# One decoder block on one core: six small steps of the parameters' load, the scan, the sinks, the top-k search and the last scaled tile take other places

## Time and profile before

| | |
|---|---|
| median of three runs | 1599.07 us (1597.56 to 1600.12) |
| the profiled execution, its own time | 1598.55 us |
| its span (first to last instruction) | 1596.8 us |
| granted TensorE clock | 0.999 |
| ACT, busy | 691.2 us, 43% |
| POOL, busy | 735.4 us, 46% |
| DVE, busy | 1256.3 us, 79% |
| DMA | 385.42 MB, mean 241 GB/s |
| instructions | 25965 |

### The profile page before, as it was taken

How to read it: one execution, slowest core, us unless ns; L and a number is a source line. 1 busy time by engine, 2 the same in 40 slices (tenths; PEclk the granted TensorE clock), 3 DMA queues, 4 the chain that set the end, 5 groups by cost and what they waited for, 6 DMA issues and landing times.

```text
span 1596.8 us, 25965 instructions
## 1 busy us (share of the span) xinstructions
PE 1582.3 (99%) x9610; PEld 1394.9 (87%) x9610; DVE 1256.3 (79%) x2491; ACT 691.2 (43%) x1003; POOL 735.4 (46%) x482
## 2 busy tenths in 40 slices
PE   9999999999999999999999999999999999999998
PEld 9887777778889999999999999999999999888886
DVE  5863655644889989999588888888888888888886
ACT  6223455534434457777443333333333333333334
POOL 4774344434556566665156444545444444422210
PEclk9999999999999999999999999999999999999999
DMA  4222121434223369997999999999999999888884
GB/s 154 87 92 80 54 67 54 147 117 145 80 80 119 110 210 324 305 328 253 320 349 378 345 342 339 349 338 344 343 348 340 344 342 320 294 312 309 304 320 169
DMA packets 151393, 385.42 MB, mean 241 GB/s; under 512 B 11792, under 2 KB 61200, under 8 KB 151184
## 3 DMA queue, kind: packets, MB, share of 16 engines
q1 hardware_dynamic: 59472, 203.54, 35.4%
q0 software_dynamic: 41472, 151.01, 27.0%
q10 hardware_dynamic: 50368, 29.89, 6.1%
HBM read 355.03 MB, written 28.84 MB: 240 GB/s over the span
## 4 chain that ended last, share of the span: by engine, by line
PE 85%; POOL 4%; issue 4%; DVE 4%; DMA 2%; ACT 1%; ACTq 0%; SPq 0%; DVEq 0%; POOLq 0%
PE ps L1490 68%; PE ps L1573 5%; PE ps L1895 4%; PE ps L1510 3%; POOL wlo L507 3%; DMA vraw<-in_v 1%; POOL score L548 1%; PE ps L1849 1%; PE ps L1707 1%; PE ps L1685 0%; PE ps L1726 0%; DMA uraw<-in_uT 0%; DVE vwlo L1342 0%; DVE mtmp L1191 0%; PE ps L1597 0%
## 5 line engine op out<-in xcount | busy, mean ns | idle before, releaser
L1490 PE MATMUL ps<-hThi,uwhi 128*128 128x352 f32 x1024 | 336.5, 329 | 2.3 <-DVE uwlo L1337 1.1
L1490 PE MATMUL ps<-hTlo,uwhi 128*128 128x352 f32 x1024 | 330.7, 323 | 0.0
L1490 PE MATMUL ps<-hThi,uwlo 128*128 128x352 f32 x1024 | 330.4, 323 | 0.0
L1490 PE MATMUL ps<-vwhi,awhi 128*128 128x512 f32 x768 | 299.5, 390 | 1.2 <-DVE awlo L1360 1.1
L1490 PE MATMUL ps<-vwlo,awhi 128*128 128x512 f32 x768 | 299.7, 390 | 0.0
L1490 PE MATMUL ps<-vwhi,awlo 128*128 128x512 f32 x768 | 299.3, 390 | 0.0
L875 ACT ACTIVATE vwhi<-vraw 128x1024 fp32r<-128x1024 f32 x128 | 135.8, 1061 | 330.2 <-PE ps L1490 294.9
L598 POOL DMA_INDIRECT rows<-in_v,gidx x128 | 147.7, 1154 | 270.2 <-DVE acc L1383 253.0
L598 POOL DMA_INDIRECT rows<-in_u,gidx x128 | 178.9, 1398 | 193.0 <-DVE rows L1376 149.3
L507 POOL TENSOR_TENSOR wlo<-raw,whi 128x1024 fp32r<-128x1024 f32 x63 | 156.0, 2476 | 222.2 <-ACT whi L642 222.1
L830 ACT ACTIVATE uwhi<-uraw 128x1024 fp32r<-128x1024 f32 x128 | 135.7, 1060 | 252.7 <-PE ps L1490 243.1
(11 more groups left out here) (332 smaller groups left out, 2872.8 us busy)
## 6 DMA issues: line engine op xcount, KB each, us to landing
uraw<-in_uT SPq DMA_DIRECT2D x128, 512.0 KB, 5.3
vraw<-in_v SPq DMA_DIRECT2D x128, 512.0 KB, 5.7
raw<-in_wstream SPq DMA_DIRECT2D x70, 512.0 KB, 3.5
gmat<-gates_dram SPq DMA_DIRECT2D x64, 384.0 KB, 6.3
gates_dram<-piece ACTq DMA_DIRECT2D x11, 2048.0 KB, 13.2
xt<-in_xT SPq DMA_DIRECT2D x8, 264.0 KB, 6.0
acc<-in_x ACTq DMA_DIRECT2D x1, 2048.0 KB, 11.4
rows<-in_u,gidx POOLq DMA_INDIRECT x128, 7.1
```

The source lines that it names most:

```text
L1490: ins = pe.matmul(dst, lhs[a], rhs[b], start=first and i == 0, stop=last and i == 2)
```

## The change

- The parameters' load goes from SP's queue, where it was third, to ACT's, where it is the first instruction.
- ACT's z stage: after tile 3, tile 4's copy out of PSUM and tile 6's high part (`z_pair(2)`, k = 0) come ahead of the sigmoid of the forget gate, k = 1 behind it.
- DVE's scan of 128 x 2112 becomes two of 128 x 1056. The first waits for `w_lo` of at least 9, the second for 10, and the maximum behind them for 11 (it was 10).
- The sink column of each attention step is written by ACT instead of DVE: the one for step 0 ahead of the loop over the steps, those for steps 1 to 15 behind the exponentials of the step before. DVE's maximum waits for it through a new semaphore, `sink_ok`.
- The sum of the halves of score 14 goes from POOL to DVE, ahead of that score's search; POOL makes tile 1's low part directly behind tile 0's, then waits for that sum, and then adds score 15.
- ACT's conversion of the indices goes from ahead of tile 4's high part to behind it, ahead of `gelu(2)`.
- `scaled(0)` goes from `v` tile 124 to 125 in DVE's loop. (The other place in which `FIN_AT` stands, in ACT's loop, L973, is unchanged.)

```
--- before.py
+++ after.py
@@ -339,7 +339,7 @@
-        names = """g_first avm_ok akx_ok ones_ok par_in sink_in acc_in fin_in consts early_in early_in1 early_hi early_lo xsq_ok xadd_ok xsum_ok sd_ok rstd_ok z_copied gate_copied yhi_ok y_ok w_hi w_lo w_used z_out
+        names = """g_first avm_ok akx_ok ones_ok par_in sink_in sink_ok acc_in fin_in consts early_in early_in1 early_hi early_lo xsq_ok xadd_ok xsum_ok sd_ok rstd_ok z_copied gate_copied yhi_ok y_ok w_hi w_lo w_used z_out
@@ -381,7 +381,6 @@
         def _(sp):
             sp.dma_start(raw[:, 0, 0:EARLY], wstream[0, :, 0:EARLY]).then_inc(S["early_in"], 16)
             sp.dma_start(xt[:, 0, :], xT[:, 0, :]).then_inc(xt_in[0], 16)
-            sp.dma_start(par[:], params).then_inc(S["par_in"], 16)
             sp.dma_start(raw[:, 1, 0:EARLY], wstream[1, :, 0:EARLY]).then_inc(S["early_in1"], 16)
             sp.dma_start(xt[:, 1, :], xT[:, 1, :]).then_inc(xt_in[1], 16)
             sp.dma_start(raw[:, 0, EARLY:D], wstream[0, :, EARLY:D]).then_inc(w_in[0], 16)
@@ -566,8 +565,8 @@
                                         ).then_inc(row_in[q % SLOTS], 16)
 
             u_split(0)
-            score_sum(RS - 2)
             u_split(1)
+            pool.wait_ge(S["s_out"], RS - 1)
             score_sum(RS - 1)
             for n in range(2, U_TOP + 1):
                 if n == U_TOP - 1:
@@ -645,6 +644,7 @@
             def spans(ap):
                 return ap.rearrange("p (b x) -> p b x", b=2)
 
+            act.dma_start(par[:], params).then_inc(S["par_in"], 16)
             act.wait_ge(poo, 1)
             act.activation(rstd[:, 0:1], eps[:], ACT.Copy)
             act.wait_ge(S["early_in"], 16)
@@ -673,8 +673,8 @@
             act.wait_ge(S["lb_max"], 1)
             act.activation(lbw[:, 3:5], lbw[:, 1:3], ACT.Exp).then_inc(S["lb_exp"], 1)
 
-            def z_pair(it, dst, shift, meta):
-                for k in range(2):
+            def z_pair(it, dst, shift, meta, slots=range(2)):
+                for k in slots:
                     own = bass.ds(it * 2 + (k - shift), 1)
                     act.wait_ge(S["w_used"], it * 2 + (k + 1))
                     if meta:
@@ -696,9 +696,11 @@
 
             z_pair(1, zm, 0, True)
 
+            z_pair(2, zr, 4, False, (0,))
             act.wait_ge(S["z_out"], 4)
             act.activation(f_z, f_z, ACT.Sigmoid).then_inc(S["f_sig"], 1)
-            z_tiles(4, 8, zr, 4, False)
+            z_pair(2, zr, 4, False, (1,))
+            z_tiles(6, 8, zr, 4, False)
             z_tiles(8, 14, zm, 4, True)
             z_tiles(14, N_Z, zr, 10, False)
 
@@ -747,6 +749,15 @@
                 act.activation(oat["hi"][:, :, tt * P:(tt + 1) * P],
                                ps[:, tt % 2, :].rearrange("p (c t) -> p c t", c=4), ACT.Copy).then_inc(S["oat_hi"], 1)
 
+            def sink_column(p):
+
+                need(act, S["aexp"], 2 * p)
+                act.activation(atsc[:, :, KEYS:KEYS + 1], sink[:].rearrange("p (s c) -> p s c", s=2)[:, :, p % 4:p % 4 + 1],
+                               ACT.Copy).then_inc(S["sink_ok"], 1)
+
+            act.wait_ge(S["sink_in"], 16)
+            act.wait_ge(S["asc_mm"], 1)
+            sink_column(0)
             for i in range(HEADS + 1):
                 if i >= 5 and i % 4 == 1:
                     attention_hi(i // 4 - 1)
@@ -754,6 +765,8 @@
                     turned(i - 1)
                 if i < HEADS:
                     exponentials(i)
+                if i + 1 < HEADS:
+                    sink_column(i + 1)
                 if i == HEADS:
                     attention_hi(TT - 1)
                 for t in gate_blocks_done(gates_before(i), gates_before(i + 1)):
@@ -880,10 +893,6 @@
                 act.activation(act_w["hi"][:, m % 2, :], prod[:, m % 2, :], ACT.Copy).then_inc(S["aw_hi"], 1)
 
             for n in range(U_TOP):
-                if n == 2:
-
-                    act.wait_ge(S["tops_ok"], RS)
-                    act.activation(top_f[:], top_i[:], ACT.Copy).then_inc(S["topf_ok"], 1)
                 if n == 13:
                     act.wait_ge(S["soft"], 1)
                     act.activation(gate[:], gate[:], ACT.Exp).then_inc(S["soft_exp"], 1)
@@ -901,6 +910,10 @@
                     act.activation(tab_ji[:, 0], ps[:, 7, P:TOK].rearrange("p (t k) -> p t k", k=P), ACT.Copy).then_inc(S["tj_ok"], 1)
                 if n < U_TOP - 1:
                     u_split(n + 2, n % 2)
+                    if n == 2:
+
+                        act.wait_ge(S["tops_ok"], RS)
+                        act.activation(top_f[:], top_i[:], ACT.Copy).then_inc(S["topf_ok"], 1)
                     gelu(n)
 
 
@@ -1036,9 +1049,12 @@
             chain.done(dve.memset(starts[:], 0.0))
             chain.done(dve.tensor_copy(halves(starts[:])[:, :, 0:1], halves(f_z)[:, :, 0:1]))
             chain.done(dve.memset(halves(f_z)[:, :, 0:1], 0.0))
-            dve.wait_ge(S["w_lo"], SCAN_AT)
-            chain.done(dve.tensor_tensor_scan(flat(decay[:]), flat(f_z), flat(starts[:]), 0.0, ALU.mult, ALU.add))
-            dve.wait_ge(S["w_lo"], SCAN_AT + 1)
+            for n in range(2):
+                own = slice(n * HH // 2, (n + 1) * HH // 2)
+                dve.wait_ge(S["w_lo"], SCAN_AT + n)
+                ins = dve.tensor_tensor_scan(flat(decay[:, own]), flat(f_z[:, own]), flat(starts[:, own]), 0.0, ALU.mult, ALU.add)
+            chain.done(ins)
+            dve.wait_ge(S["w_lo"], SCAN_AT + 2)
             chain.done(dve.tensor_scalar(decay[:], decay[:], TINY, None, ALU.max))
             chain.done(dve.reciprocal(inv[:], decay[:]))
 
@@ -1134,15 +1150,13 @@
 
             def logits(p):
 
-                lo, c = P if p < 4 else 0, p % 4
+                lo = P if p < 4 else 0
                 dve.wait_ge(S["asc_mm"], p + 1)
-                if p == 0:
-                    dve.wait_ge(S["sink_in"], 16)
                 need(dve, S["aexp"], 2 * p)
-                dve.tensor_copy(atsc[:, :, KEYS:KEYS + 1], sink[:].rearrange("p (s c) -> p s c", s=2)[:, :, c:c + 1])
                 chain.done(dve.scalar_tensor_tensor(out=atsc[:, :, lo:KEYS], in0=ps[:, 6:8, lo:KEYS], scalar=HD ** -0.5,
                                                     in1=bandmask[:, lo:KEYS].unsqueeze(1).to_broadcast([P, 2, KEYS - lo]),
                                                     op0=ALU.mult, op1=ALU.add))
+                dve.wait_ge(S["sink_ok"], p + 1)
                 dve.tensor_reduce(atstat[:, 0, :], atsc[:, :, lo:KEYS + 1], AX_X, ALU.max,
                                   negate=True).then_inc(S["amax"], 1)
 
@@ -1226,6 +1240,10 @@
 
             def set_tops(n):
                 s = n % 2
+                if n == RS - 2:
+                    dve.wait_ge(S["s_half"], n + 1)
+                    dve.tensor_tensor(score[:, s], halfscore[:, s, :, 0, :], halfscore[:, s, :, 1, :], ALU.add
+                                      ).then_inc(S["s_out"], 1)
                 dve.wait_ge(S["s_out"], n + 1)
                 for tt in range(TT):
                     ins = dve.max(top_v[:, tt, n, 0:8], score[:, s, tt, :])
@@ -1468,7 +1486,7 @@
                     dve.wait_ge(S["dots_gelu"], c + 1)
                     dve.tensor_tensor(pick_w[:, own], dots[:, own], flat_tile(gate)[:, own], ALU.mult
                                       ).then_inc(S["dots_ok"], 1)
-                if vb == FIN_AT:
+                if vb == NK - 3:
                     scaled(0)
 
             dve.wait_ge(S["acc_back"], 16 * (TT - 1))
```

1 line of the change is left out of this document (removed).

## The result

The changed kernel takes 1601.47 us in the median of 18 runs (1600.0 to 1603.42), the kernel before 1598.88 in as many (1597.0 to 1600.59). The ratio is 1.0017 with a 95% interval of 1.0011 to 1.0024: slower by 2.7 us (1.8 to 3.8). Forecast were 1600.7 and, as the likeliest of three signs, no change over 0.2%. The measured ratio lies just inside that bound, the upper end of its interval (1.0024) outside it.

A forecast was written before the change was run, and what follows sets the result against it. PE was taken as the bound, busy 1582.3 of 1596.8 us. Terms -0.2 -1.55 -0.6 +1.95 +2.2 -0.15 = +1.65 on 1598.55 gave 1600.2, or 1600.7 as a median; range 1595.4 to 1603.5.

The forecast's parts named there:

- Step 0: First attention step: DVE's maximum waits for ACT's sink column behind a gate tile, delaying PE's transposes; 1.95 us lost.
- The steps sum: U stage: PE waits for DVE's late `steps` products before adding them; 2.65 us of waiting.
- the slip: U stage: DVE's chain up to the `steps` products runs 7.6 us later, against a slack of 5.45.
- Tiles 6 and 9: Z stage: PE's waits for POOL's low parts of these two weight tiles go; 1.55 us gained.
- the last step: Last attention step: the long sink copy leaves DVE and PE's wait before 282.56 goes; 0.6 us gained.
- the sum by sharing: Alternative total if DVE and POOL shared the path and only slowed a little: slip about 2.8, sum -1.0 us.
- The halves of the scan: Z stage, DVE: each half takes about 2.2 to 2.8 us, placed around POOL's low part of tile 9.
- Rival B: U stage: additions slip between POOL's tiles, slip under 5, no 2.65 us wait for `steps`; 1598.0 us, chance 0.20.
- Start: Kernel's beginning: parameters' load issued earlier on ACT's queue lets PE begin sooner; 0.2 us gained.
- U tile 4: U stage: with the index conversion behind its high part, PE's wait for this tile goes; 0.45 us net gained.
- The tail: Kernel's end: moving the first scaled tile shortens PE's wait by 0.44, but the first addition starts only 0.15 us earlier.
- both new waits: PE's waits at attention step 0 (1.95 us) and before the `steps` sum in the u stage (2.65 us).

The follow-up runs named there:

- sink0_dve: The changed kernel with the sink column of step 0 written by DVE, the fifteen others staying on ACT: 1599.8 us, ratio 1.0006.
- sink0_ahead: The changed kernel with ACT writing sink column 0 ahead of the last gate tile's copy and high part instead of behind them: 1600.93 us, ratio 1.0009.
- sum14_pool: The changed kernel with score sum 14 back on POOL: 1597.8 us, ratio 1.0000.
- topf_first: The changed kernel with ACT's conversion of the indices back ahead of u tile 4's high part: 1601.02 us, ratio 1.0016.
- z_alone: The kernel before with the z stage's part alone (tile 4's copy and tile 6's high part before the sigmoid, scan in two halves): 1596.84 us, ratio 0.9994.
- the load's two experiments: Parameters' load back on SP's queue in the changed kernel: 1601.7 us; the load alone moved to ACT's queue in the kernel before: 1599.02 us.
- par_alone: The kernel before with the parameters' load alone moved to ACT's queue: 1599.02 us, ratio 0.9998.

## Why the prediction was right

*What the sum got right.* The places and sizes of all large terms, and by them that the losses outweigh the gains: +1.65 forecast, +3.0 in the profiled pair, +2.7 by the ratio. Step 0: 1.95 forecast, an idle of 1.88 and 1.90 in the ledger. sink0_dve shows that moving column 0 to ACT is its whole cause, sink0_ahead that the gate tile ahead of it makes 1.4 of it. The steps sum: 2.65 forecast, an idle of 2.60. Its working also held in between: searches 2.2 later, additions to 504.9 (near 505), steps products to 547.7. sum14_pool and topf_first show that the slip arises only where the additions meet POOL's tiles 4 and 5. Tiles 6 and 9: 1.55 forecast and 1.65 measured, in z_alone 1.61; the last step: 0.6 and 0.62.

*The rule on the shared port.* By the Trainium skill (SBUF — State Buffer, "SBUF: two separate sides") one of the two waits out the whole of the other. Here the first addition took 2.65 us where it took 0.67 before, and ended 0.55 behind POOL's tile 4 (499.67); the sixth took 2.54 instead of 0.34 and ended 0.22 behind tile 5 (503.51). Whichever was late was the one held (POOL's in sum14_pool). The trace agrees, and the sum by sharing (-1.0) is refuted by the ratio. The halves of the scan fit too: each began about 0.1 behind POOL's scaling of a z tile (1.3 us) and took 0.6 to 1.2 more than forecast. Rival B was half right on the way: four of the seven additions did run in the gap between the two tiles, in 1.1 us together. But the first, the sixth and the seventh were held, and the slip was 7.5 where B wanted it under 5.

*What missed.* Start, -0.2: the profiled pair showed +0.67, but the load's two experiments show no effect either way; ACT has the second raw piece anywhere from 7.8 to 8.8, which covers the term. U tile 4, -0.45: the idle of 0.40 went in full (0.28 stays where the score sum is on POOL), but the ledger's -0.96 doesn't measure it: the same stretch, 282.56 to 539.77, gives -0.96 in par_alone too, where nothing in it was changed. That is pace, and which way it went was luck. The tail: -0.15 forecast, -0.35 in the ledger. Its idle lost 0.44 as forecast; the first addition was held up by 0.12, not by 0.3. The halves of the scan, 3.4 each for 2.2 to 2.8.

*What was left out.* For step 0 the prediction says "What PE does next has been ready longer, so nothing gives it back", and for both new waits it takes the wait's own length as the cost. It can be more: behind the two new waits the clock can fall, for 1.6 us each time. The profiled execution of the changed kernel had neither fall; its +1.26 between 545 and 793 is 0.12 of restart, 0.38 of slower pace behind the sum (7.99 us for 48 products, 7.61 before, at clock 1.00), and 0.76 of pace and restarts further on that the rows do not split. The waits for low parts from 770 on are not in it: 1.21 against 1.14, and anything from 0.23 to 2.55 in the other profiles. The forecast came within 0.8 of the median since the falls and the pace are smaller than the terms that were seen. That "no change over 0.2%" came true is in part luck: the ratio is 0.0003 under the bound.

*What stays open.* The ratios of the parts alone (z -1.0, sinks +3.0, u +3.4, load -0.3) add up to 5.1 above the kernel before, the whole change to 2.7. Four intervals of 1.4 make 2.8 together (as the root of the sum of squares), so this is no contradiction, but it isn't shown either what the parts do to each other. The scaled tile was not tried alone. Where the slower pace comes from was not tried.

## What to carry to other kernels

Where PE is 99% busy, price a moved instruction by its exact place in the new queue: a 0.19 us copy cost 1.9 us because it stood behind a gate tile, and a 0.7 us addition, together with a moved conversion, 2.6 us because the two pushed seven others into a neighbour engine's tiles. Put a split-off instruction where its input is ready and nothing long stands ahead of it, and move two-input DVE work only to stretches in which POOL rests. If PE must wait about 2 us, filling the wait with products that are overwritten or never read is worth a try: it kept the clock up here, though the 0.8 us that it gave are within the intervals.
